# Four products of constants on TensorE behind the column sums of each normalisation

## The reference

```
hl = layer_norm(DEEPNORM_ALPHA * hl + m_l[2] * snake(yl), ln_g[i, 0], ln_b[i, 0])      # block 1
hl = layer_norm(DEEPNORM_ALPHA * hl + m_l[5] * sq_relu_mlp(modulate(hl, m_l[3], m_l[4]), ffn_w1[i], ffn_w2[i]), ...)
...
h = h + g1 * y                                                                         # block 2
h = h + g2 * ffn(rms_norm_2(h, norm2_g[l]) * (1 + sc2) + sh2)
```

## Time and profile before

| | |
|---|---|
| median of 3 runs | 3199.26 us (3198.19 to 3200.58) |
| profiled execution, span from first to last instruction | 3197.3 us |
| TensorE busy | 3044.7 us, 95% of the span, 13248 records |
| VectorE / ScalarE / GpSimd busy | 1338.9 / 544.4 / 107.2 us |
| share of TensorE in the chain that ended last | 90% |
| mean granted clock of TensorE | 0.975 |
| read from HBM | 428.32 MB, 134 GB/s over the span |

### The profile page before, as it was taken

One profiled execution on the slowest core, in us unless ns is written; L12 is line 12 of the kernel. 1 busy time (PEld: TensorE's weight loads), 2 busy tenths in 40 slices (PEclk: granted clock), 3 DMA queues, 4 the chain that ended last, 5 costly groups with the idle time before them and its releaser, 6 DMA issues.

```text
span 3197.3 us, 33171 instructions
## 1 busy us (share of the span) xinstructions
PE 3044.7 (95%) x13248; PEld 2060.0 (64%) x13248; DVE 1338.9 (42%) x3117; ACT 544.4 (17%) x1149; POOL 107.2 (3%) x84
## 2 busy tenths in 40 slices
PE   7999889999999999899999998999999979999999
PEld 2448444444456666788844555888446656999998
DVE  3566465467647777321031327875013342000011
ACT  0215110000033434121021221000012331000000
POOL 0000000000000000000000002343000000000000
PEclk9999999999999999999999999999999988999999
DMA  7550145566322222345521103544222011887785
GB/s 259 171 171 27 53 161 183 156 189 180 115 66 60 79 80 75 109 146 136 154 84 68 53 27 129 174 164 129 76 92 80 27 53 67 289 301 265 267 290 194
DMA packets 395321, 431.58 MB, mean 135 GB/s; under 512 B 15449, under 2 KB 307960, under 8 KB 395034
## 3 DMA queue, kind: packets, MB, share of 16 engines
q1 hardware_dynamic: 294320, 329.77, 31.8%
q10 hardware_dynamic: 100842, 99.62, 9.7%
HBM read 428.32 MB, written 1.05 MB: 134 GB/s over the span
## 4 chain that ended last, share of the span: by engine, by line
PE 90%; DVE 4%; ACT 2%; issue 1%; DMA 0%; DVEq 0%; ACTq 0%
PE bank L828 45%; PE bank L2569 10%; PE bank L2150 7%; PE bank L846 6%; PE bank L2583 4%; PE bank L854 4%; PE bank L528 2%; PE bank L1942 1%; DVE arena L573 1%; PE bank L1935 1%; PE bank L2551 1%; PE bank L2595 1%; PE bank L1539 1%; PE bank L1559 1%; PE bank L1927 1%
## 5 line engine op out<-in xcount | busy, mean ns | idle before, releaser
L828 PE MATMUL bank<-uT,slot 128*128 128x512 f32 (+2 forms) x2208 | 784.9, 512 | 0.0
L828 PE MATMUL bank<-arena,slot 128*128 128x512 f32 (+1 forms) x2016 | 694.0, 506 | 12.9 <-DVEq L2749 10.6
L828 PEld LDWEIGHTS bank<-uT,slot 128*128 128x128 f32 (+1 forms) x2208 | 416.3, 191 | 320.5 <-issue 296.8
L828 PEld LDWEIGHTS bank<-arena,slot 128*128 128x128 f32 x2016 | 386.3, 193 | 299.2 <-issue 275.1
L573 DVE SCALAR_TENSOR_TENSOR arena<-arena,sT 128x256 f32<-128x256 f32 x784 | 365.6, 520 | 7.4
L2569 PE MATMUL bank<-arena,slot 128*128 128x128 f32 x2816 | 316.2, 275 | 3.1 <-issue 2.5
L2569 PEld LDWEIGHTS bank<-arena,slot 128*128 128x128 f32 x2816 | 315.2, 192 | 5.8 <-issue 5.8
L846 PE MATMUL bank<-uT,slot 128*128 128x512 f32 (+1 forms) x448 | 180.4, 568 | 24.7 <-ACT uT L595 12.5
L2654 DVE TENSOR_TENSOR arena<-bank,halves 128x256 f32<-128x256 f32 (+1 forms) x48 | 19.3, 402 | 432.1 <-ACT halves L2615 432.1
L907 DVE SCALAR_TENSOR_TENSOR hT<-bank,mod,hT 128x256 f32<-128x256 f32 (+1 forms) x88 | 36.7, 455 | 370.6 <-PE bank L828 370.6
L846 PEld LDWEIGHTS bank<-uT,slot 128*128 128x128 f32 x448 | 93.1, 209 | 111.7 <-issue 106.4
(11 more groups left out here) (360 smaller groups left out, 2727.0 us busy)
## 6 DMA issues: line engine op xcount, KB each, us to landing
arena<-in_ada_w ACTq DMA_DIRECT2D x88, 1024.0 KB, 5.3
slot<-in_ffn_w SPq DMA_DIRECT2D x42, 2048.0 KB, 9.0
slot<-in_moe_w SPq DMA_DIRECT2D x32, 2048.0 KB, 10.0
slot<-in_moe_w SPq DMA_DIRECT2D x32, 1408.0 KB, 8.9
slot<-in_moe_w SPq DMA_DIRECT2D x16, 1536.0 KB, 9.1
slot<-in_ssd_w_in SPq DMA_DIRECT2D x32, 512.0 KB, 6.8
slot<-in_gla_w_in SPq DMA_DIRECT2D x6, 2048.0 KB, 10.3
slot<-in_ev_w_in SPq DMA_DIRECT2D x6, 2048.0 KB, 7.9
```

The lines of the kernel that those rows point to most:

```text
L828: ins = pe.matmul(bank[0:m, 0:t1 - t0], w[:, k, c0:c0 + m], x[:, k, t0:t1], start=(k == 0), stop=(k == kt - 1))
```

## The change

A helper issues four products of `one` with the first 512 columns of the constants (identity, two triangles, ones) into bank 7, with no wait and no semaphore; nothing reads the bank. `Norm.pe` calls it at its end: behind the squares' product where the norm is not the combined one, and behind the eight L723 products in the combined one.

```
+        def keep_clock(pe):
+            for _ in range(4):
+                pe.matmul(ada_rows_bank[:, :], one, const[:, 0:512], start=True, stop=True)
...
                 pe.wait_ge(*S("nsq").taken("pe", KD))
                 pe.matmul(squares[:, 0:T], one, rl[(KD - 1) % 2][:, 0:T], start=False, stop=True).then_inc(full_sem, 1)
+                if not self.rms:
+                    keep_clock(pe)
                 if self.rms:
                     bank = B.empty(pe, i + 1)
                     pe.wait_ge(*S("ctx_summed").taken("pe"))
...
                     ins.then_inc(full_sem, 1)
+                    keep_clock(pe)
```

## The result

The changed kernel takes **3177.98 us** (median of 5 runs, 3175.79 to 3183.86) against 3199.26 us (median of 5, the three of the table before and two more; 3198.19 to 3200.58): ratio 0.9935, interval 0.9923 to 0.9947. The five runs lie 8 us apart, and each time goes with its mean granted clock: 3183.86 with 0.979, 3181.06 with 0.980, 3177.98 with 0.982, 3175.90 and 3175.79 with 0.983. The profiled execution is the first of these, the slowest. Its span is 3182.0 us, 15.3 less than the span of the profile before.

The account below looks back on a forecast made before the run. TensorE was taken to bound the kernel (90% of what ended last), its clock halving around idle gaps at the norms. -15.65 + 0.65 - 0.8 = -15.8 us from 3199.26 gave 3183.4 us, range 3180 to 3189.5 for 8 in 10.

Parts of the forecast that it names:

- The helper's own cost: At the seven norms: eight records, hidden at norms 1, 2 and 7, overrunning the gaps at 3 to 6: +0.65 us.
- Norms 1 to 6, -15.65 us: Behind norms 1 to 6: no clock fall, so half of 31.29 us of busy time at half speed goes.
- Norm 7, -0.8 us: Router behind norm 7: its 8-column products partly keep full clock; between 0 and 2.5 us won, -0.8 taken.
- the term for the other low stretches: Half-speed stretches outside the changed places: no gain or loss in the sum; each could win or lose one or two us.
- Rival 1: Falls at norms 1 to 6 are shorter in timed runs, or come back elsewhere: 3189 us, chance 0.12.
- rival 2: More is won: router keeps its clock (2.5 us) and one or two other low stretches shorten: 3179 us, chance 0.08.
- Rival 4: At the norms, products of constants do not hold the clock: 3203 us (no change) to 3219 us (slower), chance 0.08.
- What the Trainium skill said: Slow products' number differs from run to run; timed runs would lose less than the profiled one as often as more.

Follow-up runs that it names:

- e1: The changed kernel run once more with no edit, on another chip's set of runs: 3178.86 us.
- e9: Kernel before, without the helper at the norms, with two products of constants filling the 1.81 us wait at SSD's start: 3199.80 us, ratio 1.0000.
- e10: Kernel before, with one product of 256 columns (0.43 us of work) added ahead of SSD's first weights: 3195.36 us, ratio 0.9990.
- e16: Kernel before, with four products of 256 columns (1.7 us of work) added ahead of SSD's first weights: 3205.07 us.
- e4: Changed kernel, with the helper's four products of 512 columns replaced by sixteen thin ones of 8 columns: 3206.86 us, ratio 1.0026 to the kernel before.
- e6: Changed kernel, with the helper at the six norms other than norm 2 only: 3181.66 us.

## Why the prediction was right and where it was wrong

- **The helper's own cost.** Right. Records 0.43 us apart, hidden at norms 1, 2 and 7, overrun at 3 to 6. From the squares' product to the first one of the next stage it takes 0.00, 0.17, 0.15 and 0.27 us longer than before at norms 3 to 6, 0.6 in all for 0.65 worked out. That an overrun is paid in full is shown with eight products (22.0 us for 18.8 worked out; the profile's low stretch at SSD's start can be part of the rest).
- **Norms 1 to 6, -15.65 us.** Right in its place: no profile of the four-product helper has a low stretch behind one of norms 1 to 6 that has the helper, and the thin products show that it is the clock and not the filled gap that counts. As a size it is one draw: the second profile of the kernel before has 3.35 + 5.79 + 5.28 + 5.72 + 5.88 + 6.06 = 32.1 us of busy time in the six stretches, so 16.0 us.

The third and fourth number of that sum are in the windows of that profile above; the other four are from these, of the same view:

```profile
391.40:394.80 3.40, 3.35 (x4) 1.52 (x5) 3.40 (x7) 1.20 (x2) 0.00 (x0) 0.50 0.00 1
896.50:903.30 6.80, 5.79 (x8) 2.63 (x9) 6.80 (x15) 4.21 (x10) 0.00 (x0) 0.50 0.00 0
...
1930.80:1937.60 6.80, 5.88 (x7) 2.52 (x8) 6.55 (x15) 4.03 (x7) 0.00 (x0) 0.50 0.30 115
2391.60:2398.40 6.80, 6.06 (x14) 4.88 (x15) 6.58 (x14) 4.10 (x7) 0.00 (x0) 0.50 0.31 117
```

- **Norm 7, -0.8 us.** The step is right and its worth can't be told: 1.1 us is won in the router in two profiles (0.6 in e1's), and with and without it the time is the same within the spread.
- **The step that failed** is the term for the other low stretches, which the sum holds at zero. Rival 1 says of them that "moved by the change they can win or lose one or two us each". The loss was priced there, and the gain only in rival 2, at 0.08, with the range ending inside it. Measured, the change gains 20 to 21 us, some 5 us more than the sum. Outside norms 1 to 6 the busy time in low stretches is 99.2 and 102.8 us in the two profiles of the kernel before and 105.0, 101.7 and 91.7 in the three of the changed one. So the first profile, with 3182.0 us of span, has no gain there at all and took 3183.86 us, about what was forecast; the third, with 3176.0, has (101.0 - 91.7)/2 = 4.6 us. The extra gain is in the faster executions, whose mean clock is higher.
- **That it went this way is in part luck.** The fall at SSD's start is one of these terms: full in both profiles of the kernel before, absent in two of the changed kernel's and half in the third. It is not a term to add, since its removal alone, by filling, won nothing (e9). What is shown is that such falls move the whole time by some 4 to 5 us in either sense, 3.9 less in e10 and 6.6 - 1.7 = 4.9 more in e16, and that the changed kernel's runs have the higher clock: 0.979 to 0.983 against 0.972 to 0.976. Why they come out better behind this change, and not worse, is not shown.
- **Rival 2**, 3179 us, named the right time and half of the reason: the router did not keep its clock, but other low stretches shortened in the faster executions. I gave it 0.08 and let the range end at 3180, just above it.
- **Rival 4** is excluded for 512 columns; with 8 columns the helper does not hold the clock.
- **What the Trainium skill said.** By its rule ("TensorE: Matmul & The Clock Gate", "What's actually happening") the count of slow products differs from run to run. I weighed it down because three runs of the kernel before lay within 2.4 us. The runs agree with the page: the busy time at half speed is 130.5 and 134.9 us in two profiles of the kernel before and 91.7 to 105.0 in three of the changed one, and the runs of the kernel before spread over 6.5 to 8.3 us on each chip, the first five of the changed one over 8.1.

That the gain goes through the clock can be read from the profiled executions. Half of the busy time in low stretches is (130.5 + 134.9)/4 = 66.4 us before and (105.0 + 101.7 + 91.7)/6 = 49.7 after, 16.7 us less, and the spans are 3197.7 and 3179.5 on average, 18.2 less. What a span holds beyond that half is 3132.0 and 3130.6 us before, and 3129.5, 3129.6 and 3130.2 after: nearly one number. Two of these three executions of the changed kernel are the slowest of their fives, so they show less than the medians do. What stays open is how the further 5 us divide among the places, and why the changed kernel's low stretches hold less as a rule; too few of its faster executions were profiled.

## What to carry to other kernels

Products of constants in a gap of TensorE pay when the gap is short enough to be filled and the work behind it is TensorE's own; take wide products (512 columns held the clock, 8 did not), leave up to 1.5 us idle rather than overrun the gap (two products left 1.3 to 1.6 us at norms 3 to 6, and the clock held there), and read the gain as half of the busy time that the low stretches hold. Do not add up the falls outside the places that are changed: they form anew in every version, and half a microsecond of work made the kernel 4 us faster while 1.7 us of it made the kernel 6.6 us slower. A single profile, or a close spread of three runs, says little about how far they can move, so keep some 5 us to either side for them in a kernel like this one, with 18 to 27 low stretches.

## What the runs showed of the hardware that was not expected

- Products of 8 columns with their weight loads, one behind the other without a gap, did not hold the clock: it fell 2.55 and 1.71 us after the first of them (e4, norms 3 and 5). Products of 512 columns over 3.6 us did hold it.
- A wait of 1.81 us made the clock fall or not by its place in time: with it beginning 31.9 us behind the last return of the clock there was a fall (five profiles of four kernels), at 32.3 and 32.4 us there was none (e10, e6), at 33.7 a short one (e16).
- One product of 256 columns added to the kernel made it 3.9 us faster in the median (interval of the ratio 0.9981 to 0.9999).
- Runs of one kernel on one chip spread over 6 to 8 us with the mean granted clock, which moves by 0.001 to 0.004 with them.
